# Expert 0's rows by one-hot products, earlier ranks, another order of the prologue

## The chip, the core and the metric

The kernel runs on one core of a Trainium2 chip. A core has engines that run their own instruction streams side by side: TensorE (PE, matrix products, with its weight loads shown apart as PEld), VectorE (DVE), ScalarE (ACT), GpSimd (POOL) and SyncE (SP), which here only issues transfers. Engines wait for each other on semaphores, and 16 DMA engines move data between main memory (HBM) and the core's SBUF. Matrix products accumulate in PSUM, which has eight banks. The metric is the time of one execution on the device, in microseconds (us); lower is better.

## What is computed

The reference is one step of a decoder layer on 512 prompt tokens and 8 sample tokens of 1024 numbers: three branches (convolution, stick-breaking attention, cross-attention to a memory), merged by gates, then a mixture of experts. The change touches the start (norm and first projections) and the experts:

```python
def rms_norm(x, g):
    xf = x.astype(jnp.float32)
    y = xf * lax.rsqrt(jnp.mean(xf * xf, axis=-1, keepdims=True) + EPS)
    return y.astype(x.dtype) * g
...
    e_logits = (hf @ w_router + b_router).astype(jnp.float32).reshape(T, N_GROUPS, EXPERTS_PER_GROUP)
    e_in = jnp.take_along_axis(e_logits, g_idx[:, None, None], axis=1)[:, 0]
    top_v, top_i = lax.top_k(e_in, TOP_K)
    gate = jax.nn.softmax(top_v, axis=-1) * jnp.take_along_axis(g_prob, g_idx[:, None], axis=1)
    expert = g_idx[:, None] * EXPERTS_PER_GROUP + top_i
...
        return (jax.nn.silu(xb @ w1[e]) * (xb @ w3[e])) @ w2[e]
```

Each token chooses one of 4 groups and in it 2 of 8 experts. There are 32 experts with w1 and w3 of 1024x512 and w2 of 512x1024, so 6 MB of float32 weights for each.

## The kernel before

Tokens are worked on in NT = 5 tiles: four of 128 prompt tokens (0 to 3) and one with the 8 sample tokens (4). D = 1024 is cut in KD = 8 slices k. Each engine has a program written out by hand, so the order of its instructions is that of the source; semaphores named in the source tie the engines together. Nothing is scheduled by a tool.

**Prologue.** SP loads the x tiles, then the first weight chunks and the small vectors; POOL makes the constants and loads page_i (the page table) over its own DMA queue, q0. For each tile in the order 4, 0, 1, 2, 3, ACT squares and sums a row (L1453) and takes the root (L1445, one tile behind the squares), DVE takes the reciprocal and scales the tile (L1807, L1808). PE turns the scaled tile by multiplying with ident (transposes, L754), ACT writes xn_hi (times norm1, rounded for the fast fp32r format) and DVE xn_lo, the rest. The projection is then a sum of three products, xn_hi by w_hi, xn_lo by w_hi and xn_hi by w_lo (three_products, L775); ACT and DVE split each weight chunk into w_hi (L1464) and w_lo (L1813). Chunks 0 and 1 are multiplied together, k by k; the transposes of slices 4 to 7 stand ahead of the products of slices 0 to 3.

**Router.** After the branches are merged and projected, the tiles go through the router in the order MERGE_TILES = 0, 1, 4, 2, 3. For each, PE turns x1 (turn_x) and multiplies by w_r (route_x, L1219), ACT writes the normed rows h_tok (scaled, L1701) and stores them to h_dram over its own queue (L1704), and DVE chooses the two experts (choose, L2205 to L2226), which ends in picked, a 0/1 row of 32 experts for each token. When the last tile is done, PE multiplies picked by triangles of ones (L1260, L1262), which gives every token's rank among those of its expert; DVE turns the ranks into positions (at_pos, one-hot over the CAP = 64 slots of an expert), and find (L1272) multiplies at_pos by pick_tok, the token numbers, so that each slot knows its token. DVE writes these as pair_row (L2266), and POOL gathers from h_dram the 128 rows of a pair of experts with an indirect DMA (gather, L702). keep_warm (L1226) are products whose result nobody reads. A second find with pick_of gives the gates of the slots; the over_ instructions on DVE and a third find (with over_pos) find tokens beyond 64 for an expert.

**Experts.** A pair's gathered rows xg are turned by PE in two halves through bank 4 (turn_rows), and DVE multiplies each half by norm2 into xg_t (rows_out, L2318). For each expert PE multiplies xg_t by w1 and w3 (up, L1304 and L1305), DVE copies that out (up_sb, L2352), PE turns it (turn_up), ACT applies the sigmoid (L1737) and DVE finishes the activation; PE multiplies by w2 (down, L1320 and L1321). ACT then scales the result by the gate: first few (L1743, for the sample tokens), then y_top (L1747); DVE makes y_rest (L2364). While the next expert runs, PE spreads the rows back to the tokens (give, L1330, by the one-hot spread that POOL writes, L711), and DVE adds them to x (L2369). The weights have three places, a, b and c, and expert n uses place n mod 3; SP issues w1 and w3 in halves of 1 MB and w2 with 2 MB as soon as the place is free (L533, L554, L558, L564). Expert 0's first loads are issued before the router ends.

## Time and profile before

| | us |
|---|---|
| runs (3) | 1096.79, 1097.74, 1098.09; median 1097.74 |
| profiled execution | 1102.6 |
| its span | 1100.8 |
| PE busy in the span | 1048.1 |

The profiled execution has a span (first to last instruction) of 1100.8 and its whole time is 1102.6. "PE busy" is the time with at least one product under way. The trace's times count from the start of the span. In the windows, PEclk is the clock that TensorE was granted, as a share of full speed (1.00 is 2.4 GHz, 0.50 is 1.2 GHz), and a DMA share of 1.00 means that all 16 DMA engines were busy. "Releaser" is what an instruction waited for last.

### The profile page before, as it was taken

What the parts mean: (1) busy time and instruction counts of PE and PEld (TensorE: products, weight loads), DVE (VectorE), ACT (ScalarE), POOL (GpSimd) and SP (SyncE); (2) the same over time, 40 slices, a digit from 0 to 9 for tenths busy, and PEclk for the clock granted to TensorE, in tenths of its full rate; (3) what the DMA queues carried; (4) which work ended last, traced back from release to release, by engine and by line L of the source; (5) the groups of instructions that cost most, each with busy time, mean ns of one, the idle gap of its engine ahead of it and who ended that gap; (6) DMA issues with size and microseconds to landing.
All of it is one profiled execution on the core that took longest, in us unless ns stands there. A gap on an engine that the chain in (4) does not pass through costs nothing.

```text
span 1100.8 us, 15991 instructions
## 1 busy us (share of the span) xinstructions
PE 1048.1 (95%) x6536; PEld 691.9 (63%) x6536; DVE 572.2 (52%) x913; ACT 307.7 (28%) x450; POOL 148.5 (13%) x179
## 2 busy tenths in 40 slices
PE   5999999999999999999998799999999999999995
PEld 4999987888867778899776344333444343433431
DVE  4312333677756855543545545556555655555555
ACT  5322211255436544322343011111111111111110
POOL 0000000001312565000000201111111011111110
PEclk9999999999999999999989799999999999999998
DMA  5622231544461243452415999999999999999962
GB/s 196 248 81 92 79 96 39 186 152 173 144 220 56 70 134 96 168 209 102 159 41 214 398 425 427 425 426 425 427 427 426 426 425 427 425 426 429 425 292 79
DMA packets 50213, 278.37 MB, mean 253 GB/s; under 512 B 7522, under 2 KB 7794, under 8 KB 29668
## 3 DMA queue, kind: packets, MB, share of 16 engines
q1 hardware_dynamic: 41332, 254.26, 57.3%
q0 software_dynamic: 6048, 16.86, 4.6%
q10 hardware_dynamic: 2768, 6.33, 1.6%
q8 instruction: 47, 0.77, 0.3%
q14 instruction: 18, 0.15, 0.0%
HBM read 274.04 MB, written 7.48 MB: 256 GB/s over the span
## 4 chain that ended last, share of the span: by engine, by line
PE 88%; DMA 4%; DVE 3%; issue 2%; POOL 1%; ACT 1%; SPq 0%; ACTq 0%; DVEq 0%; POOLq 0%
PE acc_all L775 25%; PE acc_all L1304 20%; PE acc_all L1320 10%; PE acc_all L1330 7%; PE acc_all L905 6%; PE acc_all L754 5%; PE acc_all L1153 4%; PE acc_all L836 2%; PE acc_all L955 1%; PE acc_all L1023 1%; DMA xg<-h_dram,pair_row 1%; DMA h_dram<-h_tok 1%; PE acc_all L1321 1%; DMA vals<-in_cache_mem_v 1%; DMA vals<-in_cache_v,page_row 1%
## 5 line engine op out<-in xcount | busy, mean ns | idle before, releaser
L775 PE MATMUL acc_all<-xn_hi,w_hi 128*128 128x260 f32 x832 | 173.9, 290 | 5.5 <-DVE gate_sb L1969 2.4
L775 PE MATMUL acc_all<-xn_hi,w_lo 128*128 128x260 f32 x832 | 168.6, 284 | 0.0
L775 PE MATMUL acc_all<-xn_lo,w_hi 128*128 128x260 f32 x832 | 168.1, 284 | 0.0
L2369 DVE TENSOR_TENSOR x<-x,acc_all 128x1024 f32<-128x1024 f32 x128 | 152.6, 1214 | 1.0 <-PE acc_all L1330 0.9
L775 PEld LDWEIGHTS acc_all<-xn_hi,w_hi 128*128 128x128 f32 x832 | 129.8, 190 | 14.9 <-issue 8.2
L775 PEld LDWEIGHTS acc_all<-xn_hi,w_lo 128*128 128x128 f32 x832 | 129.3, 190 | 0.0
L775 PEld LDWEIGHTS acc_all<-xn_lo,w_hi 128*128 128x128 f32 x832 | 129.3, 190 | 0.0
L711 POOL TENSOR_SCALAR spread<-tok_row,slots 128x512 fp32r<-128x512 f32 x32 | 50.1, 1566 | 380.7 <-PE acc_all L1330 380.7
L1813 DVE TENSOR_TENSOR w_lo<-w_raw,w_hi 128x1024 fp32r<-128x1024 f32 x52 | 63.4, 1221 | 67.6 <-ACT w_hi L1464 67.4
L1743 ACT ACTIVATE few<-acc_all,slots 8x512 f32<-8x512 f32 x64 | 43.4, 678 | 146.0 <-PE acc_all L1321 125.5
L1737 ACT ACTIVATE gate_h<-acc_all 128x256 f32<-128x256 f32 x32 | 12.3, 383 | 254.8 <-PE acc_all L754 254.8
L1304 PE MATMUL acc_all<-w_a,xg_t 128*64 128x512 f32 x176 | 80.4, 611 | 0.8 <-DVE xg_t L2318 0.8
L1305 PE MATMUL acc_all<-w_a,xg_t 128*64 128x512 f32 x176 | 80.4, 611 | 0.0
L2352 DVE COPY up_sb<-acc_all 128x512 f32<-128x512 f32 x32 | 22.1, 692 | 108.6 <-PE acc_all L1305 108.4
L1305 PE MATMUL acc_all<-w_b,xg_t 128*64 128x512 f32 x176 | 77.8, 595 | 0.0
L1304 PE MATMUL acc_all<-w_b,xg_t 128*64 128x512 f32 x176 | 77.8, 595 | 0.0
L2364 DVE SCALAR_TENSOR_TENSOR y_rest<-acc_all,slots,y_top 128x512 fp32r<-128x512 f32 x32 | 24.0, 751 | 93.0 <-ACT y_top L1747 93.0
L1305 PE MATMUL acc_all<-w_c,xg_t 128*64 128x512 f32 x160 | 70.8, 595 | 0.0
L1304 PE MATMUL acc_all<-w_c,xg_t 128*64 128x512 f32 x160 | 70.8, 595 | 0.0
L1330 PE MATMUL acc_all<-y_top,spread 64*128 64x512 f32 x256 | 60.9, 470 | 4.0 <-DVE x L2369 2.2
L1330 PEld LDWEIGHTS acc_all<-y_top,spread 64*128 64x128 f32 x256 | 24.0, 183 | 61.4 <-issue 28.5
L1472 ACT ACTIVATE proj<-acc_all 128x520 f32<-128x520 f32 (+1 forms) x28 | 16.9, 604 | 147.2 <-PE acc_all L775 141.1
(365 smaller groups left out, 1854.8 us busy)
## 6 DMA issues: line engine op xcount, KB each, us to landing
w_a<-in_w SPq DMA_DIRECT2D x44, 1024.0 KB, 16.4
w_b<-in_w SPq DMA_DIRECT2D x44, 1024.0 KB, 17.3
w_c<-in_w SPq DMA_DIRECT2D x40, 1024.0 KB, 17.8
w_raw<-in_w_in SPq DMA_DIRECT2D x52, 512.0 KB, 3.6
w_a<-in_w SPq DMA_DIRECT2D x11, 2048.0 KB, 17.4
w_b<-in_w SPq DMA_DIRECT2D x11, 2048.0 KB, 18.9
w_c<-in_w SPq DMA_DIRECT2D x10, 2048.0 KB, 20.4
w_br<-in_w_branch SPq DMA_DIRECT2D x24, 256.0 KB, 4.7
```

Of the source, the lines that this page charges most:

```text
L711: pool.tensor_scalar(spread[n % 2][:, :], tok_row[:, :], slot_tok[:, n:n + 1], None, ALU.is_equal).then_inc(spread_ok, 1)
L754: return pe.transpose(out, in_, ident[0:k, 0:k])
L775: mm = pe.matmul(out[:, a, :], w[:, slot, k, :], x[:, k, a * HALF_TOK:(a + 1) * HALF_TOK], start=first, stop=last)
L905: mm = pe.matmul(out[:, a, :], w, x[:, a * HALF_TOK:(a + 1) * HALF_TOK], start=begin, stop=end)
L1153: return pe.matmul(bank(MERGE_BANKS[i][half]), m[:, k, tok(tt)], w[:, k, half * 512:(half + 1) * 512], start=first, stop=last)
L1304: pe.matmul(bank(5)[0:CAP, :], lhs, w1_sb[w][:, k, :], start=(k == 0), stop=(k == KD - 1))
L1305: mm = pe.matmul(bank(5)[CAP:P, :], lhs, w3_sb[w][:, k, :], start=(k == 0), stop=(k == KD - 1))
L1320: pe.matmul(bank(7)[0:CAP, :], act_t[:, c, :], w2_sb[w][:, c, 0:DE], start=(c == 0), stop=(c == CW - 1))
L1330: mm = pe.matmul(bank(2 * pair + half), spread[hot][at, tok(t)], y[at, :], start=first, stop=not first)
L1743: act.activation(few[n // QUADS % 2][half][strip:strip + NB, :], bank(7)[at, :], ACT.Copy, scale=slot_gate[at, n:n + 1]).then_inc(few_in, 1)
L1813: dve.tensor_tensor(w_lo[:, slot, :, :], w_raw[:, slot, :, :], w_hi[:, slot, :, :].bitcast(F32), ALU.subtract).then_inc(split_lo, 1)
L2369: dve.tensor_tensor(x1[:, t, :], x1[:, t, :], bank(2 * pair, 2), ALU.add).then_inc(back_ok, 1)
```

## The change

What it does, engine by engine:

- **Rows of expert 0.** hot is a one-hot of slot against token for expert 0 alone. PE multiplies the rows h_tok, which lie in SBUF, by hot (hot_rows) and gets expert 0's rows already turned in banks 0 and 4; DVE multiplies by norm2 into xg_t. Expert 0 waits for row_sb and no more for the gather. Rows 0 to 63 of xg_t are filled this way; for expert 1 the pair's gathered rows are turned as before, but after expert 0's down products.
- **Ranks in two parts.** The ranks of the first four tiles (in ROUTE_TILES' order 4, 0, 1, 2) are multiplied before the last tile is chosen (rank_early), those of tile 3 after it (rank_late); slots, positions and find are cut in the same way.
- **Stores and gathers.** The last tile's row store goes from ACT's queue to SP's, ahead of w3[1]. The second half of w3 and w1 of place c waits for row_ps as well, since h_tok lies there. gather(1) waits until the second find (ids_ps 2), because at_pos now lies in its buffer.
- **Moves.** The second find stands behind expert 0's up products, the third behind its down products; the over_ instructions on DVE stand beside expert 0, and few_hot behind rows_out(0, 1). turn_rows(1, 1) and its rows_out stand at the end of expert 1 instead of in the middle of it. keep_warm is removed.
- **Prologue.** page_i is loaded after all x tiles are scaled. ACT's root follows each square at once, the last tile is scaled in two halves, chunk 1's split comes after slice 3, the products of chunk 0 for slices 0 to 3 come first, each followed by the transposes of slice k + 4, and then those of chunk 1. PE multiplies ident by itself (warm_up) 10 times at the start, 2 times behind each of the first three tiles and 5 times ahead of the first product.

The semaphores x1_ld and route_ld became one (late_ld); three new ones are h_ok (rows scaled), row_ps (late hot products) and row_sb. The diff, cut to its core, in the order SP, POOL, PE, ACT, DVE, with the common indentation taken off:

```diff
...
 sp.wait_ge(wo_ps, 2 * NT)
 load_up(0, 0, w1_sb, w1_d)
+sp.wait_ge(h_ok, NT)
+sp.dma_start(h_dram[tok(MERGE_TILES[NT - 1]), :], h_tok[:, MERGE_TILES[NT - 1], :]).then_inc(h_st, 16)
 load_up(1, 1, w3_sb, w3_d)
...
 sp.wait_ge(h_st, 16 * NT)
+sp.wait_ge(row_ps, 2)
 load_up(2, 2, w3_sb, w3_d)
...
-pool.dma_start(page_i[:, :], io["page_table"].rearrange("b j -> (b j)").partition_broadcast(P)).then_inc(page_ld, 16)
...
+pool.wait_ge(xn_ok, NT)
+pool.dma_start(page_i[:, :], io["page_table"].rearrange("b j -> (b j)").partition_broadcast(P)).then_inc(page_ld, 16)
 pool.wait_ge(rows_ok, 1)
...
 gather(0)
-gather(1)
 pool.wait_ge(ids_ok, 2)
 spread_block(0)
 spread_block(1)
...
-pool.wait_ge(dest_ok, 3)
+pool.wait_ge(ids_ps, 2)
+gather(1)
+pool.wait_ge(dest_ok, OVER_SET)
...
+def warm_up(times):
+    for _ in range(times):
+        pe.matmul(bank(0)[:, 0:P], ident[:, :], ident[:, :], start=True, stop=True)
+pe.wait_ge(consts, 1)
+warm_up(10)
...
 for tt in range(NT - 1):
     pe.wait_ge(xn_ok, tt + 2)
     for k in range(4):
-        mm = turn(bank(4 + k)[:, tok(tt)], x_in[:, tt, k * P:(k + 1) * P], P)
+        mm = turn_tile(tt, k)
         if tt == NT - 2:
             mm.then_inc(xt_ps, 1)
+    if tt < NT - 2:
+        warm_up(2)
...
+warm_up(5)
 pe.wait_ge(split_lo, 1)
-pe.wait_ge(xt_lo, 1)
-for k in range(KD):
+pe.wait_ge(xn_ok, NT + 1)
+for k in range(4):
     pe.wait_ge(xt_lo, k + 2)
-    if k + 4 < KD:
-        for tt in range(NT - 1):
-            mm = turn(bank(4 + k)[:, tok(tt)], x_in[:, tt, (k + 4) * P:(k + 5) * P], P)
-        mm.then_inc(xt_ps, 1)
     three_products(0, k, acc_pair(0))
-    pe.wait_ge(split_lo, 2)
+    for tt in range(NT - 1):
+        mm = turn_tile(tt, k + 4)
+    mm.then_inc(xt_ps, 1)
+pe.wait_ge(split_lo, 2)
+for k in range(4):
+    three_products(1, k, acc_pair(2))
+for k in range(4, KD):
+    pe.wait_ge(xt_lo, k + 2)
+    three_products(0, k, acc_pair(0))
     mm = three_products(1, k, acc_pair(2))
 mm.then_inc(w_used, 2)
...
-keep_warm(3)
...
-o = bank(1)[:, 0:(NT + 1) * NE]
-pe.matmul(o, tri_bf[:, :], picked[:, :, :], start=True, stop=False, skip_group_check=True)
-for back in range(1, NT + 1):
-    mm = pe.matmul(o[:, back * NE:], ones_bf[:, :], picked[:, 0:NT + 1 - back, :], start=False, stop=(back == NT),
-                   skip_group_check=True)
-mm.then_inc(rank_ps, 1)
...
-keep_warm(1)
-pe.wait_ge(dest_ok, 1)
-find(at_pos, lambda n, r, c: pick_tok[0:n, r, c, :], NE, bank(3))
-keep_warm(2)
-pe.wait_ge(dest_ok, 2)
-find(at_pos, lambda n, r, c: pick_of[0:n, r, c, :], NE, bank(2))
-keep_warm(2)
...
+def rank_early():
+    o = bank(1)
+    pe.matmul(o[:, 0:LAST * NE], tri_bf[:, :], picked[:, 0:LAST, :], start=True, stop=False, skip_group_check=True)
+    for back in range(1, NT + 1):
+        n = min(LAST, NT + 1 - back)
+        mm = pe.matmul(o[:, back * NE:(back + n) * NE], ones_bf[:, :], picked[:, 0:n, :], start=False, stop=False,
+                       skip_group_check=True)
+    mm.then_inc(rank_ps, 1)
...
+def rank_late():
+    o = bank(1)
+    pe.matmul(o[:, LAST * NE:NT * NE], tri_bf[:, :], picked[:, LAST, :], start=False, stop=False,
+              skip_group_check=True)
+    pe.matmul(o[:, NT * NE:(NT + 1) * NE], ones_bf[:, :], picked[:, LAST, :], start=False, stop=True,
+              skip_group_check=True).then_inc(rank_ps, 1)
...
+def hot_rows(half, tiles):
+    for kk in range(KD // 2):
+        k = KD // 2 * half + kk
+        for r in tiles:
+            tt = ROUTE_TILES[r]
+            n = rows(tt)
+            mm = pe.matmul(bank(4 * half)[:, kk * CAP:(kk + 1) * CAP], h_tok[0:n, tt, k:D:KD], hot[0:n, r, :],
+                           start=(kk == 0 and r == 0), stop=(r == LAST), skip_group_check=True)
+    return mm
...
+early, late = range(LAST), range(LAST, NT)
+merge_out(4, 1, range(KD // 2, KD))
+route_x(4, 0)
+pe.wait_ge(pick_ok, LAST)
+rank_early()
+turn_x(4, 1)
+route_x(4, 1)
+pe.wait_ge(dest_ok, HOT_EARLY)
+pe.wait_ge(h_ok, LAST)
+hot_rows(0, early)
+hot_rows(1, early)
+pe.wait_ge(dest_ok, POS_EARLY)
+pe.wait_ge(pick_ok, NT)
+rank_late()
+pe.wait_ge(pick_ok, NT + 1)
+find_ids(early)
+pe.wait_ge(dest_ok, HOT_LATE)
+pe.wait_ge(h_ok, NT)
+for half in range(2):
+    hot_rows(half, late).then_inc(row_ps, 1)
+pe.wait_ge(dest_ok, POS_LATE)
+find_ids(late).then_inc(ids_ps, 1)
...
-turn_rows(0, 0)
-turn_rows(0, 1)
 for n in range(NE):
...
-    if j == 0:
+    if n >= 1:
         pe.wait_ge(xgt_sb, 2 * p + 2)
-    if n >= 1:
         pe.wait_ge(up_ok, n)
-    up_and_gate(n % WS, p % 2, j, n // WS + 1)
+    up_and_gate(n % WS, p % 2, j, n // WS + 1, first=(n == 0))
     if n >= 1:
         give(n - 1, (0, 1))
     else:
-        pe.wait_ge(dest_ok, 3)
-        find(over_pos, lambda m, r, c: over_in[0:m, r, c, :, :].rearrange("p a b -> p (a b)"), 2 * EXTRA, bank(0))
+        pe.wait_ge(dest_ok, GATED)
+        find(at_pos, lambda m, r, c: pick_of[0:m, r, c, :], NE, bank(2)).then_inc(ids_ps, 1)
...
-    if n + 2 < NE:
+    if n == 1:
+        turn_rows(1, 0)
+    elif 2 <= n < NE - 2:
...
     down(n % WS, n // WS + 1, n)
+    if n == 0:
+        pe.wait_ge(dest_ok, OVER_SET)
+        find(over_pos, lambda m, r, c: over_in[0:m, r, c, :, :].rearrange("p a b -> p (a b)"), 2 * EXTRA,
+             bank(0)).then_inc(ids_ps, 1)
+        turn_rows(0, 0)
+        turn_rows(0, 1)
     if 1 <= n < NE - 1:
         give(n - 1, (3,))
+    if n == 1:
+        turn_rows(1, 1)
...
     act.activation(junk[0:n, :], x_in[0:n, t, :], ACT.Square, accum_out=ss[0:n, t:t + 1]).then_inc(sumsq_ok, 1)
-    if i >= 1:
-        root(i - 1)
-root(NT - 1)
+    if i == NT - 1:
+        act.wait_ge(xst_f, 1)
+        act.activation(xn_hi[:, :, SEQ:TOK], xst_tmp[:, :, :], ACT.Copy).then_inc(xt_hi, 1)
+    root(i)
...
 split_chunk(0)
-act.wait_ge(xst_f, 1)
-act.activation(xn_hi[:, :, SEQ:TOK], xst_tmp[:, :, :], ACT.Copy).then_inc(xt_hi, 1)
-split_chunk(1)
 act.wait_ge(norm_ld, 16)
 for k in range(KD):
+    if k == 4:
+        split_chunk(1)
     act.wait_ge(xt_ps, k + 1)
...
-    act.dma_start(h_dram[tok(tt), :], h_tok[0:n, tt, :]).then_inc(h_st, 16)
+    act.activation(h_tok[0:n, tt, :], x1[0:n, tt, :], ACT.Copy, scale=rs2[0:n, i:i + 1]).then_inc(h_ok, 1)
+    if i < NT - 1:
+        act.wait_ge(h_ok, i + 1)
+        act.dma_start(h_dram[tok(tt), :], h_tok[0:n, tt, :]).then_inc(h_st, 16)
...
-mean_square(0)
 for i, t in enumerate(START_TILES):
     n = rows(t)
-    if i + 1 < NT:
-        mean_square(i + 1)
+    mean_square(i)
...
-    dve.tensor_scalar(x_in[0:n, t, :], x_in[0:n, t, :], rs[0:n, t:t + 1], None, ALU.mult).then_inc(xn_ok, 1)
+    if i < NT - 1:
+        dve.tensor_scalar(x_in[0:n, t, :], x_in[0:n, t, :], rs[0:n, t:t + 1], None, ALU.mult).then_inc(xn_ok, 1)
+    else:
+        for half in range(2):
+            at = slice(half * D // 2, (half + 1) * D // 2)
+            dve.tensor_scalar(x_in[0:n, t, at], x_in[0:n, t, at], rs[0:n, t:t + 1], None, ALU.mult).then_inc(xn_ok, 1)
+    if i == NT - 2:
...
+def hot_slots(r0, r1, part):
+    dve.wait_ge(rank_ps, part + 1)
+    at, n = slice(r0, r1), r1 - r0
+    link(dve.scalar_tensor_tensor(out=hot_rank[:, at], in0=picked[:, at, 0], scalar=-float(NO_TOKEN),
+                                  in1=rank[:, at, 0], op0=ALU.mult, op1=ALU.add))
+    dve.tensor_tensor(hot[:, at, :], bc(hot_rank[:, at].unsqueeze(2), [P, n, CAP]),
+                      bc(pos_low[:, :].unsqueeze(1), [P, n, CAP]), ALU.is_equal).then_inc(dest_ok, 1)
...
+def rank_picked(r0, r1):
+    at, n = slice(r0, r1), r1 - r0
+    link(dve.tensor_tensor(pick_of[:, at, :, :], bc(rank[:, at, :].unsqueeze(2), [P, n, 2, NE]), pick[:, at, :, :],
+                           ALU.mult))
...
+hot_slots(0, LAST, 0)
+rank_picked(0, LAST)
 dve.wait_ge(sumsq_ok, NT + 2 + 6)
 dve.scalar_tensor_tensor(out=rs2[:, 4:5], in0=ss2[:, 4:5], scalar=EPS * D, in1=ss2_b[:, 0:1], op0=ALU.add,
                          op1=ALU.add).then_inc(ms_ok, 1)
+rank_sum(0, LAST)
 scale2(2, slice(4, 5))
+position(0, LAST)
 choose(4)
...
-dve.tensor_tensor(pick_tok[:, :, :, :], pick[:, :, :, :], bc(tok_f[:, :].unsqueeze(2).unsqueeze(3), choice), ALU.mult)
+dve.tensor_tensor(pick_tok[:, :, :, :], pick[:, :, :, :], bc(tok_f[:, :].unsqueeze(2).unsqueeze(3), choice),
+                  ALU.mult).then_inc(pick_ok, 1)
+hot_slots(LAST, NT, 1)
+rank_picked(LAST, NT)
+rank_sum(LAST, NT)
+position(LAST, NT)
...
+for half in range(2):
+    ks = slice(KD // 2 * half, KD // 2 * (half + 1))
+    dve.wait_ge(row_ps, half + 1)
+    if half == 0:
+        dve.wait_ge(lg_ps, NT)
+        dve.wait_ge(lg_max, 1)
+    dve.tensor_tensor(xg_t[:, 0, ks, 0:CAP], bank(4 * half)[:, 0:KD // 2 * CAP].rearrange("p (k t) -> p k t", k=KD // 2),
+                      bc(norm2_pk[:, ks].unsqueeze(2), [P, KD // 2, CAP]), ALU.mult).then_inc(row_sb, 1)
...
     else:
+        over_first()
+    dve.wait_ge(sig_ok, n + 1)
+    if n >= 1:
+        dve.wait_ge(y2_ps, n)
+    act_out(2 * n)
+    if n == 0:
+        dve.wait_ge(ids_ps, 2)
+        dve.tensor_copy(slot_gate[:, 0:NE], bank(2)[:, 0:NE]).then_inc(ids_ok, 1)
+        over_rest()
+        rows_out(0, 0)
+        rows_out(0, 1)
         dve.wait_ge(ids_ps, 3)
         link(rows_found(PAIRS, EXTRA // 2, bank(0)))
...
-    if n + 2 < NE:
...
+    elif n == 1:
+        rows_out(1, 0)
+    elif n + 2 < NE:
         rows_out(n // 2 + 1, n % 2)
...
     y_rest_out(slot_gate[:, n:n + 1])
     if 1 <= n < NE - 1:
         added(n - 1, (3,))
+    if n == 1:
+        rows_out(1, 1)
...
```

On PE, from the end of the router to expert 0, these stood in a row before (xg_168 is a gathered pair; w13_ld0a the first halves of w1 and w3 in place a):

```order
L1219 MATMUL acc_all<-w_r,x_t_163 128x36 [waits ht_sb]
L1226 MATMUL acc_all<-x_105,ident 128x512 x3
L1260 MATMUL acc_all<-picked,tri_bf 128x192 [waits pick_ok]
L1262 MATMUL acc_all<-picked,ones_bf 128x160
L1272 MATMUL acc_all<-pick_tok,at_pos 64x32 [waits dest_ok]
L1272 MATMUL acc_all<-pick_of,at_pos 64x32 [waits dest_ok]
L754 MATMUL acc_all<-ident,xg_168 128x128 [waits xg_ld0]
L754 MATMUL acc_all<-ident,xg_168 128x128 [waits xgt_sb]
L1304 MATMUL acc_all<-w_a,xg_t 64x512 [waits w13_ld0a,xgt_sb]
```

On PE at the same place, these stand there now (L1316 are the hot products):

```order
L1294 MATMUL acc_all<-picked,tri_bf 128x128 [waits pick_ok]
L1249 MATMUL acc_all<-w_r,x_t_163 128x36 [waits ht_sb]
L1316 MATMUL acc_all<-hot,h_tok 128x64 [waits h_ok,dest_ok]
L1316 MATMUL acc_all<-hot,h_tok 128x64 x31
L1304 MATMUL acc_all<-picked,tri_bf 128x32 [waits pick_ok,dest_ok]
L1283 MATMUL acc_all<-pick_tok,at_pos 64x32 [waits pick_ok]
L1316 MATMUL acc_all<-hot,h_tok 128x64 x7
L1283 MATMUL acc_all<-pick_tok,at_pos 64x32 [waits dest_ok]
L1365 MATMUL acc_all<-w_a,xg_t 64x512 [waits w13_ld0a,row_sb]
L1283 MATMUL acc_all<-pick_of,at_pos 64x32 [waits dest_ok]
```

The transposes of the gathered rows are gone from the place ahead of expert 0's first up product, the hot products stand there instead, and the gates' find has moved behind the up products.

On DVE, in expert 1, these stood in a row before (xg_t is the half of the next pair's rows, x_105 is x1, y_rest that of expert 1):

```order
L2318 TENSOR_TENSOR xg_t<-acc_all,norm_pk 128x512 [waits xgt_ps]
L2369 TENSOR_TENSOR x_105<-x_105,acc_all 128x1024 [waits back_ps] x2
L2364 SCALAR_TENSOR_TENSOR y_rest<-acc_all,slots,y_top 128x512 [waits top_ok]
L2369 TENSOR_TENSOR x_105<-x_105,acc_all 128x1024 [waits back_ps]
L2352 COPY up_sb<-acc_all 128x512 [waits upt_ps,up_ps]
```

On DVE at the same place, these stand there now:

```order
L2448 TENSOR_TENSOR xg_t<-acc_all,norm_pk 128x512 [waits xgt_ps]
L2476 TENSOR_TENSOR x_105<-x_105,acc_all 128x1024 [waits back_ps] x2
L2471 SCALAR_TENSOR_TENSOR y_rest<-acc_all,slots,y_top 128x512 [waits top_ok]
L2476 TENSOR_TENSOR x_105<-x_105,acc_all 128x1024 [waits back_ps]
L2448 TENSOR_TENSOR xg_t<-acc_all,norm_pk 128x512 [waits xgt_ps]
L2459 COPY up_sb<-acc_all 128x512 [waits upt_ps,up_ps]
```

A second xg_t, the other half of expert 2's and 3's rows, now stands behind y_rest of expert 1 and one more addition.

On SP, at the router's end, these transfers now stand in a row; the store to h_dram is the new one, and the last row has row_ps as a second wait:

```order
L539 DMA w_a<-in_w 128x2048 [waits wo_ps]
L560 DMA h_dram<-h_tok 128x1024 [waits h_ok]
L539 DMA w_b<-in_w 128x2048 x2
L562 DMA w_b<-in_w 128x4096
L539 DMA w_c<-in_w 128x2048 x2
L539 DMA w_c<-in_w 128x2048 [waits row_ps,h_st]
```

The store stands between expert 0's w1 and expert 1's w3, so everything from w3[1] on is issued behind it.

## Rows read from the trace of the kernel before

**Rows 1.** The page, part 1: busy us (share of the span) xinstructions of each engine.

```profile
PE 1048.1 (95%) x6536; PEld 691.9 (63%) x6536; DVE 572.2 (52%) x913; ACT 307.7 (28%) x450; POOL 148.5 (13%) x179
```

**Rows 2.** Chain of waits, 590 to 630: start us, us, what.

```profile
595.37 9.12 DMA h_dram<-h_tok
...
605.35 9.20 DMA xg<-h_dram,pair_row
...
617.73 0.70 DVE xg_t L2318
...
619.60 0.85 PE acc_all L1304
...
624.20 0.43 PE acc_all L1304
```

**Rows 3.** Windows, 614 to 616: PE, PEld, DVE, ACT, POOL busy (x), PEclk, DMA share, GB/s.

```profile
614.00:616.00 2.00, 1.12 (x4) 0.71 (x4) 0.17 (x1) 0.00 (x0) 0.00 (x0) 0.50 0.98 404
```

**Rows 4.** Tiles w_b, w_c: duration ns min/median/max, first and last start us, forms.

```profile
L1304 PE MATMUL acc_all<-w_b,xg_t x176: 592/592/643, 634.8 to 1074.8; 128*64 128x512 f32 x176
...
L1304 PE MATMUL acc_all<-w_c,xg_t x160: 592/592/643, 649.1 to 1046.1; 128*64 128x512 f32 x160
```

**Rows 5.** DMA issues, 1010 to 1027: xcount, KB each, median us from issue to landing.

```profile
w_a<-in_w SPq DMA_DIRECT2D x1, 2048.0 KB, 28.9
```

**Rows 6.** Timeline, 1000 to 1070: start us, us, engine, line, operation [idle before <-releaser].

```profile
1024.72 0.33 SPq L564 DMA_DIRECT2D w_a<-in_w  x1
...
1064.09 0.61 PE L1320 MATMUL acc_all<-w_a,act_t 128*64 128x512 f32 x1 [0.31 <-DVE act_t L2361]
```

**Rows 7.** Timeline, prologue (0 to 36), ACT, DVE and PE.

```profile
10.05 1.06 ACT L1453 ACTIVATE junk<-x_in 128x1024 f32<-128x1024 f32 x1 [2.47 <-DMA x_in<-in_x_prompt]
...
15.91 1.23 DVE L1813 TENSOR_TENSOR w_lo<-w_raw,w_hi 128x1024 fp32r<-128x1024 f32 x1
...
18.68 0.78 PE L775 MATMUL acc_all<-xn_hi,w_hi 128*128 128x260 f32 x2
...
19.26 0.64 PE L775 MATMUL acc_all<-xn_lo,w_hi 128*128 128x260 f32 x2
...
23.00 0.40 PE L775 MATMUL acc_all<-xn_hi,w_lo 128*128 128x260 f32 x2
```

**Rows 8.** Windows, 7.0 to 7.5, columns as in rows 3.

```profile
7.00:7.50 0.50, 0.08 (x1) 0.11 (x2) 0.27 (x1) 0.50 (x3) 0.00 (x0) 1.00 2.21 141
```

**Rows 9.** DMA queues, 6 to 8: packets, MB, share of 16 engines.

```profile
q0 software_dynamic: 20, 0.01, 51.6%
```

**Rows 10.** Timeline, router's end (590 to 626).

```profile
593.92 1.08 PE L1219 MATMUL acc_all<-w_r,x_t 128*128 128x36 f32 x8 [0.69 <-ACT x_t L1686]
...
598.77 0.18 DVE L2226 TENSOR_TENSOR picked<-pick 128x32 bf16<-128x32 bf16 x1
...
601.48 1.47 PE L1272 MATMUL acc_all<-pick_tok,at_pos 8*64 8x32 f32 x40 [1.05 <-DVE at_pos L2260]
```

**Rows 11.** DMA issues, 560 to 600, columns as in rows 5.

```profile
w_a<-in_w SPq DMA_DIRECT2D x2, 1024.0 KB, 5.9
```

**Rows 12.** Windows, DVE's work between pair_row and over_pos, columns as in rows 3.

```profile
603.00:612.50 9.50, 6.83 (x48) 2.92 (x48) 8.58 (x30) 0.00 (x0) 5.15 (x4) 0.82 1.01 425
618.30:623.30 5.00, 4.83 (x12) 1.48 (x14) 4.62 (x14) 0.00 (x0) 0.00 (x0) 0.50 1.03 437
```

**Rows 13.** Timeline, POOL and DVE at 607 to 611.

```profile
607.71 3.13 POOL L711 TENSOR_SCALAR spread<-tok_row,slots 128x512 fp32r<-128x512 f32 x2
607.80 2.21 DVE L2300 TENSOR_TENSOR scan<-scan 128x32 f32<-128x32 f32 x4
```

**Rows 14.** Timeline, behind expert 1's last down product (648 to 652).

```profile
648.58 1.38 ACT L1743 ACTIVATE few<-acc_all,slots 8x512 f32<-8x512 f32 x2 [4.48 <-PE acc_all L1321]
...
650.71 0.75 DVE L2364 SCALAR_TENSOR_TENSOR y_rest<-acc_all,slots,y_top 128x512 fp32r<-128x512 f32 x1 [2.59 <-ACT y_top L1747]
...
651.38 1.21 DVE L2369 TENSOR_TENSOR x<-x,acc_all 128x1024 f32<-128x1024 f32 x1
```

175 lines of the change are left out of this document (89 added, 86 removed).

## The prediction

> **What bounds the kernel now.** I read the page first: TensorE (PE) is busy for 1048.1 of 1100.8 us [rows 1], so time can only come out of the few places where PE stands or runs at its lower clock. The chain of waits names the largest. The last row store is issued at 595.37 and needs 9.12 us, because it queues behind weights; the gather that reads it back needs another 9.20; then come transposes and two multiplications by the norm weights, the second 0.70 [rows 2]. While PE waited it idled, and the windows show what followed: a granted clock of 0.50, the lower of its two levels (1.2 of 2.4 GHz) [rows 3]. At that level a pair of expert products takes 0.85 us, later 0.42 to 0.43 [rows 2]. The first six pairs of expert 0 run so, which costs 6 x 0.43 = 2.5 us. Experts 1 and 2 begin at 634.8 and 649.1 [rows 4], so an undisturbed expert takes 14.3.
>
> Second, the weights: could they refuse an earlier expert stage? Expert 30's w2 is issued at 1024.72 [rows 6] and takes 28.9 [rows 5], so it is there at 1053.6; its first use is at 1064.09 [rows 6]. That slack of 10.5 us is the most that the expert stage can be moved ahead. Third, the prologue: the first product begins at 18.68, and products run at the lower level until about 22.8 (0.64 us for two that overlap, later 0.40) [rows 7].
>
> **Prologue.** The square of x tile 2 waited 2.47 us for its DMA and began at 10.05 [rows 7], while ACT had been ready at 7.58. In that stretch transfers fell to 141 GB/s [rows 8], and q0, which holds only the page table's load then, took 51.6% of the 16 engines with 20 packets [rows 9]. The change issues that load after the last x tile is scaled; its first reader, a gather of key pages, comes late in the attention, so the delay is hidden. The Trainium skill speaks against a gain here: "DMA: Bandwidth & Descriptors", section "SWDGE vs HWDGE vs iDMA", says that each DMA engine goes round-robin between the queues of either kind, so 20 small packets should hardly delay x. By that rule the 1.75 us below would drop out and the whole sum would be 8.0 instead of 9.7; the rows of this place show the opposite.
>
> With ACT's root now placed right after each square, I put tile 2's square at 8.3, 1.75 sooner. Chunk 1's split no longer stands before the first xn_lo (1.23 [rows 7]), and the transposes of k = 4 no longer stand before the first product (0.7, the gap from the last xn_lo to 18.68). Some 0.2 more comes from scaling the last tile in halves. So the first product starts at 18.68 - 1.75 - 1.23 - 0.7 - 0.2 = 14.8. Not all is kept: the 0.46 us of those transposes return behind the first product, and pacing by xn_lo (ACT 0.69, DVE 0.75 for each k) I estimate at 0.3. The clock decides the rest. Before, 4.1 us of products passed before the rise, costing 2.0. The warm-ups put some 1.35 us of work straight ahead of the first product, so I let the rise come after 2.75 us of products, which cost 1.35. Gain: 3.9 - 0.46 - 0.3 + 0.65 = **3.8**. If products run at the full level at once it is 5.1. The trace has no warm-ups; 3 us of transposes before 18.68 did not raise the clock, so the other end is that the lower level lasts through the four interleaved k (2.45 us each, against 1.2): 1.3 slower. Everything up to the router is paced by PE, so this carries on.
>
> **Router to expert 0** (times of the trace of before). The early ranks are six small bf16 products, about 0.5, at 592. On DVE the early slots (two instructions, estimated 0.7) and rank_picked (estimated 0.42, four of the five tiles) come ahead of the reciprocal and push the last choose, which ended at 598.95 [rows 10], by 0.2 to 0.4. The early hot products are 32 of 128x64: from eight router products of 36 columns in 1.08 [rows 10] I take 0.135 each, 4.3 us, with 3.4 as the other end. They run from 595.0 to 599.3, beside choose, which hides them. Then follow pick_tok 0.49, slots of the last tile 0.4, eight late hot products 1.0, and two halves of the norm multiplication at 0.42 (of which PE waits for the first only): expert 0 starts at **601.75** instead of 618.48. Its w1 halves land 5.9 us after 590.94 [rows 11], so at 596.9, which is no limit. Store and gather leave the path: the store now stands ahead of w3[1] on SP and waits for h_ok at 595.9; behind it are queued w3[1], w2[1] and w1[2], a gap of at most 0.5 us in a stream that still holds w1[0]; the gather lands at about 612.4. The gather of experts 2 and 3 waits for a product after expert 0's up and lands at 620, used at 629.
>
> **Expert 0 to 1.** What was 16.7 sooner is not kept. The up products take 16 x 0.43 = 6.9, to 608.65, but DVE's routing work now stands beside expert 0 instead of before it, and expert 1 needs xg_t, which comes behind it. In the trace this work is the 9.5 and 5.0 us of two windows [rows 12]; less few_hot (1.1, moved behind), plus up_out 0.69 and act_out 1.13, it takes 15.2 from 602.3, so over_pos ends at 617.5 (616.65 if the scan steps beside POOL's spread run at their usual pace). Then find 1.47 [rows 10], and two times transposes 0.6 and multiplication 0.70 through one bank, with gaps: expert 1 starts at **621.8** instead of 634.8, 13.0 sooner. A rule of the skill bears on the same row: beside two POOL spreads (3.13) four scan steps took 2.21 on DVE [rows 13], some 1.3 more than such a step costs elsewhere. "SBUF — State Buffer", section "Who interferes with whom", says that a DVE instruction with two SBUF inputs and a GpSimd one that reads SBUF exclude each other wholly; by that, up to 3.13 instead would be lost, expert 1 would start at 623.0, and the sum would be 1.2 smaller. The row shows less.
>
> **Expert 1 to 2: a new wait.** Expert 2 needs the second half of its pair's rows, whose transposes now stand at the end of expert 1, and on DVE their multiplication stands behind y_rest of expert 1 and a 1.21 us addition [rows 14]. y_rest needs ACT's two "few" (1.38) and y_top, all after the last down product. In the trace of before, those steps lie beside expert 2: 648.58 to 651.38 + 1.21 = 652.6 [rows 14]; with 0.70 for the multiplication and gaps, expert 2's first product comes 4.95 us after the end of down(1), where it was 0.65. So 4.3 of the 13.0 are given back: expert 2 starts at 640.4, **8.7** sooner. During the stall PE idles for about 4 us, as it did ahead of expert 0 in before, where the lower level followed. I take one such fall at its measured price of 2.5, and 0.3 for the spread of the terms: **5.9** of 8.7. With no fall 8.5 to 9; with two (one more behind expert 0) 3.4. All is under the 10.5 that the weights allow. From expert 2 on nothing differs.
>
> **Sum.** 3.8 + 5.9 = 9.7. The profiled execution took 1102.6, so it would be 1092.9; the median of the runs is 1097.74, which gives **1088.0**.
>
> **Rivals.** (1) *The clock holds*: prologue 5.1, experts 8.5, together 13.6, 1084.1. For it: expert 0 now follows the router's products almost without a gap; against it: the stall before expert 2. (2) *The clock falls twice, or rises late in the prologue*: 3.4 from the experts and between -1.3 and 1 from the prologue, 2.1 to 4.4 in all: 1093.3 to 1095.6. For it: the transposes that raised nothing. (3) *Slower*: the lower level holds from the hot products on. They would take 32 x 0.28 = 9.0 instead of 4.3 (4.7 later), and the up products of expert 0 13.8 instead of 6.9, to 620.3; with both finds (1.5 each), turning and activating (1.5), down (3.4) and the two bank turns (2.9), expert 1 starts at 631.1; its up products take another 6.9 more and the stall 4.3: expert 2 at 631.1 + 14.3 + 6.9 + 4.3 = 656.6, 7.5 later than before. With the late prologue (1.3) that is 1106.5. It decides once more than 12.5 us (8.7 + 3.8) are lost; against it, PE is busy nearly throughout from 594 to 608. (4) *The change does not do what it says*: expert 0 still waits for weights; then only the prologue is left, 1094; the 5.9 us to landing [rows 11] speak against it. (5) *The page table's load did not hold x up*: x comes no sooner, the 1.75 drops out, 9.7 - 1.75 = 7.95 is left: 1089.8, inside the forecast's spread.
>
> **How the numbers follow.** Forecast, with (5) in it, 0.56; (1) 0.17; (2) 0.19; (3) 0.04; (4) 0.04. The range leaves out the slow case, half of (2)'s upper side and what lies below (1): 1083 to 1094.5. A measurement of this kernel tells 0.2% (2.2 us) from no change. Faster than that holds the forecast, (1), (4) and most of (2): 0.92; within it, the top of (2): 0.04; slower, (3): 0.04.
>
> **What would show it.** Right: tile 2's square near 8.3 and the first product near 14.8; two 128x260 products falling from 0.64 to 0.40 by 17.5; expert 0 starting 16.7 + 3.8 sooner, expert 1 16.8, expert 2 some 10 to 12.5; ahead of expert 2 PE idle for about 4 us with DVE's xg_t as its releaser. Wrong: a granted clock of 0.50 under the hot products, PE waiting for a weight DMA in expert 0 or the last experts, or an x tile as late as before.

## The result: 0.8% slower, where 0.9% faster was forecast

The changed kernel took 1105.34 us (median of 4 runs, 1104.60 to 1106.99); the kernel before took 1097.91. The ratio is 1.0079, with an interval of 1.0061 to 1.0097. The profiled execution took 1105.24 with a span of 1103.4, so this time it stands at the median; the profiled execution of before stood 4.9 above its own.

TensorE is busier than in [rows 1], in part 1 of the page of the changed kernel (busy us, share, instructions):

```profile
PE 1065.0 (97%) x6644; PEld 715.9 (65%) x6644; DVE 573.7 (52%) x923; ACT 307.7 (28%) x450; POOL 149.0 (14%) x180
```

17 us more for 108 more instructions: what was added is dear, and it isn't waiting. The up products of the three weight places show from where on the time is lost (w_a holds expert 0, w_b expert 1, w_c expert 2; ns min/median/max, first and last start; compare [rows 4]):

```profile
L1365 PE MATMUL acc_all<-w_a,xg_t x176: 592/592/1094, 612.7 to 1062.8; 128*64 128x512 f32 x176
L1365 PE MATMUL acc_all<-w_b,xg_t x176: 592/592/643, 633.1 to 1077.1; 128*64 128x512 f32 x176
L1365 PE MATMUL acc_all<-w_c,xg_t x160: 592/592/643, 651.6 to 1048.4; 128*64 128x512 f32 x160
```

Place a in the kernel before:

```profile
L1304 PE MATMUL acc_all<-w_a,xg_t x176: 592/592/1115, 618.5 to 1060.5; 128*64 128x512 f32 x176
```

Expert 0 begins 5.8 sooner than in the profile of before (612.7 against 618.48), expert 1 only 1.7 sooner, expert 2 begins 2.5 later. Forecast were 20.5, 16.8 and 12.5 sooner (the prologue's 3.8 included). From expert 2 on nothing differs, as the prediction said.

The prologue is not at fault. The square of x tile 2, the first two products and the copy of the first chunk, from the timeline:

```profile
7.75 1.04 ACT L1521 ACTIVATE junk<-x_in 128x1024 f32<-128x1024 f32 x1
...
14.04 0.48 PE L800 MATMUL acc_all<-xn_hi,w_hi 128*128 128x260 f32 x2 [0.27 <-DVE xn_lo L1905]
14.36 0.40 PE L800 MATMUL acc_all<-xn_lo,w_hi 128*128 128x260 f32 x2
...
27.55 0.60 ACT L1541 ACTIVATE proj<-acc_all 128x520 f32<-128x520 f32 x1 [6.03 <-PE acc_all L800]
```

Against [rows 7], the square starts 2.3 sooner, the first product 4.6 sooner, and two products take 0.40 from the second on where they took 0.64: the clock is up at once. The first chunk is copied out at 27.55, in before at 33.62:

```profile
33.62 0.60 ACT L1472 ACTIVATE proj<-acc_all 128x520 f32<-128x520 f32 x1 [4.58 <-PE acc_all L775]
```

The loss stands in the chain of waits behind the router (start us, us, what):

```profile
588.01 18.26 PE acc_all L1316 x64
606.32 1.99 PE acc_all L1283 x32
608.32 4.00 PE acc_all L1316 x16
...
613.79 0.85 PE acc_all L1365
...
617.34 0.43 PE acc_all L1365
...
627.87 0.83 DVE over_pos L2443
...
651.60 0.64 PE acc_all L1365
```

L1316 are the hot products. The early ones hold PE for 18.26 us, where 4.3 were forecast; the late ones take 4.00, where 1.0 was forecast. The store and the gather [rows 2] are gone from the chain, as intended, but they took 18.3 of it, and the products that replace them take 22.3. The windows give the clock there (columns as in [rows 3]):

```profile
588.00:590.00 2.00, 2.00 (x9) 1.88 (x8) 1.67 (x9) 1.70 (x2) 0.00 (x0) 0.58 1.00 422
...
600.00:604.00 4.00, 4.00 (x16) 3.63 (x15) 0.00 (x0) 0.00 (x0) 0.00 (x0) 0.50 1.00 424
608.00:610.00 2.00, 2.00 (x14) 1.94 (x12) 0.00 (x0) 1.29 (x2) 0.00 (x0) 0.50 0.01 4
648.00:651.00 3.00, 0.20 (x2) 0.01 (x1) 1.94 (x3) 1.00 (x2) 1.23 (x1) 1.00 1.05 445
```

PE counts as busy without a gap and yet runs at the lower level, from 588.3 to 615.6. In the stall ahead of expert 2 (the last row) it is the reverse: PE stands and the clock holds. At 608 to 610 the transfers have stopped too, since w3[2] now waits for the hot products; in 600 to 612 their share is 0.57, in before 1.01. No product later waited for a weight.

### The profile page after: what moved, and what is told of

It reads as the page before. It is cut to its first block, busy times and chain, and to the rows that moved or that the text cites. A ratio compares the mean times of both kernels' runs of the same rounds, so it can differ in the third digit from the quotient of the medians.

```text
span 1103.4 us, 16224 instructions
## 1 busy us (share of the span) xinstructions
PE 1065.0 (97%) x6644; PEld 715.9 (65%) x6644; DVE 573.7 (52%) x923; ACT 307.7 (28%) x450; POOL 149.0 (14%) x180
## 4 chain that ended last, share of the span: by engine, by line
PE 89%; DVE 4%; DMA 2%; ACT 2%; issue 2%; POOL 1%; ACTq 0%; SPq 0%; DVEq 0%; POOLq 0%
PE acc_all L800 25%; PE acc_all L1365 20%; PE acc_all L1381 10%; PE acc_all L1391 7%; PE acc_all L935 5%; PE acc_all L767 5%; PE acc_all L1183 4%; PE acc_all L866 2%; PE acc_all L1316 2%; PE acc_all L985 1%; DMA vals<-in_cache_mem_v 1%; PE acc_all L1053 1%; PE acc_all L1382 1%; PE acc_all L1249 1%; DMA vals<-in_cache_v,page_row 1%
## 5 line engine op out<-in xcount | busy, mean ns | idle before, releaser
L1805 ACT ACTIVATE gate_h<-acc_all 128x256 f32<-128x256 f32 x32 | 12.3, 383 | 246.5 <-PE acc_all L767 246.5
## 6 DMA issues: line engine op xcount, KB each, us to landing
w_a<-in_w SPq DMA_DIRECT2D x44, 1024.0 KB, 14.9
w_c<-in_w SPq DMA_DIRECT2D x10, 2048.0 KB, 16.6
```

## Experiments

**The reference point.** The kernel before, unchanged, was run once more, since its profiled execution was 4.9 above its median and the prediction's sum was made against that execution.

> The kernel before, unchanged, for a second profile. The profiled execution that the prediction read took 1102.6 us, 4.7 us above the median of the runs (1097.9). Theory 1: that execution was an unlucky one, in which TensorE's granted clock lay at its lower level through the first part of expert 0; most executions have it at the full level there, so a second profile shows a span near 1096 with expert 0 at 0.43 us per pair from its first pair on. Theory 2: the lower level at expert 0 belongs to every execution and the profile itself costs the 4.7 us: span near 1100.8 again, first pairs of expert 0 at 0.85 us.

Measured: 1097.69, ratio 0.9994 (0.9977 to 1.0011), span 1095.6. The square of x tile 2 in its timeline, and the up products of w_b:

```profile
8.78 1.06 ACT L1453 ACTIVATE junk<-x_in 128x1024 f32<-128x1024 f32 x1 [1.30 <-DMA x_in<-in_x_prompt]
```

```profile
L1304 PE MATMUL acc_all<-w_b,xg_t x176: 592/592/643, 632.6 to 1072.5; 128*64 128x512 f32 x176
```

The lower clock under expert 0 is there again (610.8 to 621.0), so both expectations fell: neither a missing fall nor a fixed span explains the 4.9. The same program differs by execution in two places. Tile 2's wait was 1.30 this time, 2.47 before, and the first chunk came 1.6 sooner. From the last instruction on DVE to the end of the span it took 1.9, before 4.8. All further comparisons of times inside the span use this profile where it says so.

**The prologue alone.** Before, with the new prologue and nothing else of the change.

```diff
+pe.wait_ge(consts, 1)
+warm_up(10)
...
+pool.wait_ge(xn_ok, NT)
+pool.dma_start(page_i[:, :], ...)
...
-            root(i - 1)
+        root(i)
```

> The kernel before with the new prologue alone (page table's load after the x tiles, root right after each square, warm-ups, products of chunk 0 first); routing and experts as before. In the changed kernel the two chunks ended at 27.5 us instead of 33.6. Theory 1: everything from there to the router is paced by TensorE, so the 6.1 us carry to the end: 1091.8 us. Theory 2: a later stage is paced by transfers (key pages, values, or the experts' weights) and gives the gain back: 1096 to 1098 us.

Measured: 1091.58, ratio 0.9935 (0.991 to 0.996). The first products run at the full level (14.87 0.40, below). The first chunk is out at 28.07, against 32.03 in the second profile of before, and expert 0 starts at 611.1 against 616.5; here are the up products of place a, first with the new prologue, then in that profile:

```profile
L1322 PE MATMUL acc_all<-w_a,xg_t x176: 592/592/1116, 611.1 to 1053.5; 128*64 128x512 f32 x176
```

```profile
L1304 PE MATMUL acc_all<-w_a,xg_t x176: 592/592/1115, 616.5 to 1058.2; 128*64 128x512 f32 x176
```

The time is the first theory's 1091.8. By the medians the prologue brings some 6.5 us (by the interval 4.4 to 9.9), more than the 3.8 of the forecast; by these two traces it brings 4.0 at the first chunk and 4.7 at the last instruction on DVE. The rest of the change costs 13.8.

**Where the prologue's gain is from.** First its warm-ups left out, then the page table's load put back to its old place, each in the kernel with the prologue alone.

```diff
-pe.wait_ge(consts, 1)
-warm_up(10)
...
-        if tt < NT - 2:
-            warm_up(2)
...
-    warm_up(5)
```

> pro_only without the warm-up products. Theory 1: the warm-ups are what raises the granted clock ahead of the first product (in the changed kernel every product runs at the full level); without them the first products run at 0.64 us a pair again for some 3 to 4 us and the transposes ahead of them at the lower level too, and the end comes 1.5 to 2.5 us later: 1093 to 1094 us. Theory 2: the earlier x tiles and the closer order raise it as soon: 1091.6 us.

Measured: 1094.8, ratio 0.9979 (0.995 to 1.0008). The second pair of products, without warm-ups and with them (one line of each timeline):

```profile
14.70 0.64 PE L779 MATMUL acc_all<-xn_lo,w_hi 128*128 128x260 f32 x2
```

```profile
14.87 0.40 PE L788 MATMUL acc_all<-xn_lo,w_hi 128*128 128x260 f32 x2
```

Without them the products start 0.4 sooner (14.12), at the lower level, and the first chunk comes out at 29.68 instead of 28.07. By the medians the warm-ups are worth 3.2 of the 6.5 us, a little more than the first theory expected. But the two intervals overlap, and the traces don't show it at the end. The 1.6 us are down to 0.2 at 129 us: PE falls to the lower level at about 120 us in both, for 6.8 us with the warm-ups and 3.4 without. Expert 0 then starts 1.0 sooner without them (with them at 611.1, above):

```profile
L1312 PE MATMUL acc_all<-w_a,xg_t x176: 592/592/1115, 610.1 to 1052.4; 128*64 128x512 f32 x176
```

Its span is longer (1092.7 against 1090.9) only by what follows the last instruction on DVE, 2.9 us more. So the warm-ups raise the clock at the first products; what of it reaches the end is not shown.

```diff
+pool.dma_start(page_i[:, :], ...).then_inc(page_ld, 16)
 pool.iota(row_f[:, :], ...)
...
-pool.wait_ge(xn_ok, NT)
-pool.dma_start(page_i[:, :], ...).then_inc(page_ld, 16)
```

> pro_only with the page table's load back at its old place, ahead of the x tiles' arrival. Theory 1: this load held up x tiles 2 and 3 (in the kernel before the square of tile 2 waited 2.47 us for its transfer); tile 2 comes at 10 again instead of 7.75 and all of the prologue is about 2 us later: 1093.5 us. Theory 2: the x tiles were late for another reason, and the load costs nothing here: 1091.6 us.

Measured: 1091.23, ratio 0.994 (0.9922 to 0.9958), the same as without this edit. The squares of x tiles 2 and 3 in its timeline:

```profile
8.05 1.06 ACT L1470 ACTIVATE junk<-x_in 128x1024 f32<-128x1024 f32 x1
...
10.38 1.06 ACT L1470 ACTIVATE junk<-x_in 128x1024 f32<-128x1024 f32 x1 [0.76 <-DMA x_in<-in_x_prompt]
```

With the page table's load at its old place tile 2 needed no wait, and tile 3 one of 0.76. In the time of the whole kernel the load's place makes no difference that can be measured, as the second theory said. But that theory's reason does not hold: the transfers show that the load does hold x up. Their rate in 40 equal slices of 2 to 9 us, first with the load at its old place, then with it moved:

```profile
GB/s 0 117 23 23 164 211 94 187 515 351 398 398 421 398 421 421 515 398 398 375 257 398 492 421 445 424 401 351 331 228 108 53 47 47 47 94 47 25 140 259
```

```profile
GB/s 0 70 47 0 47 234 164 281 351 445 492 398 375 398 398 375 445 445 468 445 351 398 421 374 468 445 445 445 375 398 421 374 445 445 408 314 425 468 445 374
```

Between 7 and 9 us the mean is 98 to 159 GB/s in all three profiles with the load at its old place (both of before and this one), and 395 to 418 in all eleven with it moved. Which x tile is caught differs: tile 2 waited 2.47 and 1.30 in the two profiles of before, tile 3 0.76 here, where the first product came 0.46 later than with the load moved (15.01 against 14.55).

**The last row store alone.** The prologue, and the last store issued from SP ahead of w3[1].

```diff
+    sp.wait_ge(h_ok, 1)
+    sp.dma_start(h_dram[tok(MERGE_TILES[NT - 1]), :], h_tok[:, MERGE_TILES[NT - 1], :]).then_inc(h_st, 16)
     load_up(1, 1, w3_sb, w3_d)
```

> pro_only with one part of the routing change: the last tile's row store is issued by SP ahead of expert 1's w3 and not from ACT's queue; gather, ranks and experts as before. In pro_only the store took 8.65 us and was there at 597.4; the gather was issued at 598.28, while the row numbers that it needs were ready at 596.7. Theory 1: the store was only some 0.7 us later than those numbers, so its own 9 us were mostly hidden beside choosing and ranking, and the gather's 8.9 us stay: at most 1 to 1.5 us, 1090 to 1091.6 us. Theory 2: the store's 9 us and, by less queueing, part of the gather's stood on the path: 4 us or more, 1087.5 us or less.

Measured: 1088.16, ratio 0.9908 (0.9889 to 0.9928); the interval overlaps that of the prologue alone. The chain of waits of the prologue alone, then that with the store moved:

```profile
588.75 8.65 DMA h_dram<-h_tok
...
598.28 8.92 DMA xg<-h_dram,pair_row
```

```profile
595.88 0.17 DVE pair_row L2295
...
597.08 8.99 DMA xg<-h_dram,pair_row
```

The store has left the chain, and the router's own work has taken its place, so the gather is issued only 1.2 sooner; expert 0 begins at 610.0 instead of 611.1. The medians say 3.4, the starts of expert 0 say 1.1: how much the store's place is worth stays open between these, as the time lies between the two expectations.

**The early hot products left out.** The changed kernel without them, so that expert 0's rows of tiles 0, 1, 2 and 4 are missing.

```diff
...
-    hot_rows(0, early)
-    hot_rows(1, early)
```

> The changed kernel without the 32 early hot products (tiles 4, 0, 1 and 2 are left out of expert 0's rows; all else runs). In the changed kernel they fill TensorE from 588.0 to 606.3. Theory 1: they are the cost that the prediction put at 4.3 us; without them the last choose (picked at 591.7) sets the pace and expert 0 starts at 597 to 600 instead of 612.7: 1105.3 - 13 to -16 = 1089 to 1092 us. Theory 2: what is late is the lower clock that sets in at 588 whatever runs there, and the chain behind it; then at most half of that comes, 1097 to 1101 us.

Measured: 1090.46, ratio 0.9918 (0.9881 to 0.9954): 14.9 us off the changed kernel, and expert 0 starts at 598.2 instead of 612.7. That is the time expected, and it settles where the time went:

```profile
L1363 PE MATMUL acc_all<-w_a,xg_t x176: 592/592/1094, 598.2 to 1052.8; 128*64 128x512 f32 x176
L1363 PE MATMUL acc_all<-w_c,xg_t x160: 592/592/1061, 639.6 to 1038.4; 128*64 128x512 f32 x160
```

It also shows how little the rest of the routing change is worth: the prologue alone took 1091.58. Against that kernel expert 0 starts 12.9 sooner here, but expert 1 follows 21.3 later (there 16.6) and expert 2 another 20.1 (there 14.3), so that expert 2 starts only 2.4 sooner (639.6 against 642.0). The run doesn't yet say why 32 products take 18 us.

**Is it the clock?** Three products of 128 x 512 straight ahead of the hot products, to raise it.

```diff
     pe.wait_ge(h_ok, LAST)
+    for _ in range(3):
+        pe.matmul(bank(5), ident[:, :], x1[:, 0, 0:512], start=True, stop=True)
     hot_rows(0, early)
```

> The changed kernel with three of the old keep-warm products (128x512, whose result nobody reads; 2.8 us at the full level) put straight ahead of the early hot products. In the changed kernel the granted clock falls at 588.1, when these begin, and stays at 0.50 until 615.4. Theory 1: the hot products themselves hold the lower level, so it sets in a few us later and lasts as before: 1104 to 1107 us. Theory 2: the gaps between 584.7 and 587.9 made it fall, and with the gaps filled it stays at the full level: 32 products in 9 us instead of 18.3, and the late ones, finds and first up products faster too: 1105.3 + 2.8 - 9.2 - 4.8 = 1094 us.

Measured: 1109.86, ratio 1.0108 (1.0085 to 1.0131), some 3 us above what the first theory expected; its kind was right. Its line of early hot products in the timeline, and windows of L1316 alone (us, PE busy (x), PEld busy (x), PEclk, DMA share, GB/s):

```profile
587.74 18.06 PE L1316 MATMUL acc_all<-hot,h_tok 8*128 8x64 f32 x64
```

```profile
588.00:592.00 4.00, 4.00 (x16) 3.80 (x16) 1.00 1.01 426
594.00:598.00 4.00, 4.00 (x15) 3.53 (x15) 0.50 0.98 412
```

The clock was raised and held until 593.4. A window counts every instruction that reaches into it: 16 in four microseconds at the full level, 15 at the lower. So the clock doesn't price these instructions. Nor do they keep it up: with PE busy throughout, it fell in the midst of them and stayed low until 617.3. In this run's profile the lower level also set in behind the stall ahead of expert 2, for some 6 us, which the profile of the changed kernel was spared; whether the 3 us above the expectation are these is not shown.

**Is it the number of instructions?** The rows and the one-hot blocks were given the type fp32r, so that low bits of the rows are lost.

```diff
-        h_tok = place("h_tok", "ys", 0, [NT, D])
+        h_tok = place("h_tok", "ys", 0, [NT, D], F32R)
...
-        hot = place("hot", "ys", 20480, [NT, CAP])
+        hot = place("hot", "ys", 20480, [NT, CAP], F32R)
...
```

> The changed kernel with h_tok and hot written in the rounded fp32r format, in which a product is one instruction and not two (the rows of all experts lose their low bits by that). In the changed kernel each instruction of the hot products takes 0.285 us at the lower level, and there are 64 for the 32 early products. Theory 1: the count of instructions is the cost: 32 in 9.1 us, the late ones in 2 instead of 4: 1105.3 - 9.2 - 2 = 1094 us, less if the clock rises sooner. Theory 2: what costs is loading each 128x128 block once, whatever the format: the time of an instruction doubles, 1104 to 1106 us.

Measured: 1093.55, ratio 0.9952 (0.9928 to 0.9977), as expected if instructions are the price. Early and late hot products:

```profile
587.11 9.83 PE L1316 MATMUL acc_all<-hot,h_tok 8*128 8x64 f32 x32
...
598.95 2.12 PE L1316 MATMUL acc_all<-hot,h_tok 128*128 128x64 f32 x8
```

The same 32 and 8 products are now 32 and 8 instructions instead of 64 and 16, and take half as long. A plain fp32 product is two instructions here.

**Is it the loaded block's step?** A hot product loads 128 columns h_tok[:, k:D:KD], every eighth value. Here it loads neighbouring ones, so that expert 0's columns are permuted; the three products of 512 columns stay.

```diff
...
-                        mm = pe.matmul(bank(4 * half)[:, kk * CAP:(kk + 1) * CAP], h_tok[0:n, tt, k:D:KD], hot[0:n, r, :],
+                        mm = pe.matmul(bank(4 * half)[:, kk * CAP:(kk + 1) * CAP], h_tok[0:n, tt, k * P:(k + 1) * P], hot[0:n, r, :],
...
```

> hot_warm with one change: the block of h_tok that is loaded for a hot product is 128 neighbouring numbers of a row and not every eighth (so expert 0's rows come out with their columns permuted). In hot_warm the 64 instructions came every 0.28 us on average and every 0.24 at the closest, at the full clock level as at the lower one, and each load took 0.334 us; the router's products, whose blocks lie together, came every 0.12 us at the full level. Theory 1: the step of 32 bytes between the loaded numbers sets the pace; without it the early products take 8 to 11 us instead of 18.1 and expert 0 starts 7 to 11 us sooner: 1109.9 - 7 to -11 = 1099 to 1103 us. Theory 2: the step does not matter, the products are paced by something else: 17 us or more again, 1108 us or more.

Measured: 1102.82, ratio 1.0067 (1.0043 to 1.0092), within the first theory's range. Two of that theory's steps fell short all the same: the early products took 13.1 us where 8 to 11 were expected, and expert 0 starts 4.5 sooner than with the step, not 7 to 11. The rest of the gain lies behind it: expert 2 starts 5.8 sooner, and the stretch at the lower level that follows is shorter. Its weight loads, then those of the changed kernel and those of the router in the kernel before (ns min/median/max), each from its trace:

```profile
L1316 PEld LDWEIGHTS acc_all<-hot,h_tok x80: 181/288/337, 588.5 to 606.8; 128*128 128x128 f32 x64, 8*128 8x128 f32 x16
```

```profile
L1316 PEld LDWEIGHTS acc_all<-hot,h_tok x80: 307/334/337, 587.9 to 611.8; 128*128 128x128 f32 x64, 8*128 8x128 f32 x16
```

```profile
L1219 PEld LDWEIGHTS acc_all<-w_r,x_t x80: 88/192/338, 568.4 to 594.7; 128*128 128x128 f32 x64, 128*8 128x8 f32 x16
```

And windows of L1316 with neighbouring columns, at either level of the clock:

```profile
589.00:593.00 4.00, 4.00 (x30) 3.60 (x30) 1.00 1.03 417
594.00:598.00 4.00, 4.00 (x17) 3.53 (x17) 0.50 1.04 438
```

At the full level 30 instructions stand where 16 stood with the step; at the lower level the two are near each other, 17 and 15. So the step takes away what the full clock would give, and either of them alone, step or lower level, makes an instruction dear. The early hot products went from 18.06 to 13.11 us because the clock held for their first 4.7 us; then it fell here too (593.1).

**The wait ahead of expert 2.** The changed kernel, with the second half of the next pair's rows turned before the last quarter of down(1) and multiplied earlier on DVE.

```diff
-    down(n % WS, n // WS + 1, n)
+    down(n % WS, n // WS + 1, n, between=(lambda: turn_rows(1, 1)) if n == 1 else None)
...
-    if n == 1:
-        turn_rows(1, 1)
...
+    if n == 1:
+        added(0, (1,))
+        rows_out(1, 1)
+        added(0, (2,))
```

> The changed kernel with one thing undone in another form: the second half's transposes for experts 2 and 3 stand ahead of the last quarter of expert 1's down products, and their multiplication on DVE between the two additions of expert 0's rows, so expert 2 no longer waits for y_rest of expert 1. Theory 1: the 3.4 us of waiting and the rest of the 18.5 us between the first products of experts 1 and 2 go down to 14.3 to 15: 1105.3 - 4 = 1101.3 us. Theory 2: expert 2 is then late for another reason, w3 of place c, whose load waits for the last hot products: still 17 us or more between them, 1104 us or more.

Measured: 1102.0, ratio 1.0037 (1.0019 to 1.0055). Expert 2's up products:

```profile
L1365 PE MATMUL acc_all<-w_c,xg_t x160: 592/592/643, 647.8 to 1044.8; 128*64 128x512 f32 x160
```

Expert 1 starts at 632.6, so expert 2 follows 15.2 later, in the changed kernel 18.5, and the time is that expected. The stall of 3.3 us is avoidable, and 3.3 by the medians is what it cost.

**A better form.** The operands change places: the one-hot block (now 64 slots of expert 0 and 64 of expert 1) is loaded, and the rows stream 512 wide. Four early tiles and two halves are 8 products instead of 32, there is no step in the loaded block, and both experts' rows come from SBUF, so the first gather goes. The result is copied to xg_0, turned and multiplied as gathered rows are. DVE's count of full experts stands ahead of it, and the turns ahead of expert 2 as in the run before.

```diff
-                for kk in range(KD // 2):
-                    ...
-                        mm = pe.matmul(bank(4 * half)[:, kk * CAP:(kk + 1) * CAP], h_tok[0:n, tt, k:D:KD], hot[0:n, r, :],
+                for r in tiles:
+                    ...
+                    mm = pe.matmul(bank(4 * half), hot[0:n, r, :, :].rearrange("p a b -> p (a b)"),
+                                   h_tok[0:n, tt, half * 512:(half + 1) * 512],
...
-            gather(0)
...
+            dve.wait_ge(row_ps, 1)
+            dve.tensor_copy(xg[0][:, 0:512], bank(0)).then_inc(row_sb, 1)
```

> Another form of the same idea on the new prologue: hot has the 128 slots of experts 0 and 1 and is the operand that is loaded, the rows h_tok are the one that streams, 512 numbers wide, two products for each tile; the result is the gathered form of the pair, copied out by DVE and ACT, turned and multiplied by norm2 like any pair; the gather of that pair is left out, and the transposes for experts 2 and 3 stand as in rows_mid. Theory 1: ten products of 0.94 us (as the keep-warm products of that form took at the full level), eight of them beside the last choose; expert 0 starts at 600 to 602 instead of 612.7, expert 1 17 us later, expert 2 14.5 after that: 651.6 - 632.5 = 19 sooner than in the changed kernel, 1086 to 1087 us. Theory 2: the weights' transfers or a fallen clock take half of that back: 1091 us or more.

Measured: 1082.21, ratio 0.9853 (0.983 to 0.9875), some 4 us better than expected. Its products in the timeline, and their loads:

```profile
584.88 6.97 PE L1313 MATMUL acc_all<-h_tok,hot 8*128 8x512 f32 x8
...
591.83 5.61 PE L1313 MATMUL acc_all<-h_tok,hot 8*128 8x512 f32 x12
```

```profile
L1313 PEld LDWEIGHTS acc_all<-h_tok,hot x20: 181/190/337, 584.9 to 596.4; 128*128 128x128 f32 x16, 8*128 8x128 f32 x4
```

Twenty instructions in 12.6 us move the rows of two experts, where eighty in 22.3 moved those of one. The wide ones lift the clock themselves: 8 in 6.97 at the lower level, then 12 in 5.61 at the full one. Experts 0, 1 and 2 start at 600.1, 615.9 and 631.0, expert 2 15.9 sooner than in the second profile of before. Against the prologue alone that is 11.0 at expert 2 and 9.4 by the medians. What each of the parts brings (the exchanged operands, both experts' rows, the gather left out, the order on DVE, the turns ahead of expert 2) was not measured apart.

One addition: two short products that nobody reads, of 128 and 320 columns, ahead of the early ranks and behind the last tile's turns, to keep the clock up.

```diff
     route_x(4, 0)
+    pe.matmul(bank(5)[:, 0:128], ident[:, :], x1[:, 0, 0:128], start=True, stop=True)
...
     turn_x(4, 1)
+    pe.matmul(bank(0)[:, 0:320], ident[:, :], x1[:, 0, 0:320], start=True, stop=True)
```

> pair_rows with two short products that nobody reads, of 128 and 320 columns, in the two gaps of TensorE ahead of the early ranks and behind the last tile's transposes (0.27 and 0.69 us in pair_rows). In pair_rows the granted clock lies at 0.50 from 584.2 to 591.0, under the first of the wide hot products. Theory 1: the gaps made it fall; filled, the level holds and 6.8 us of products take 3.4 less: 1079 us. Theory 2: the fall comes from what ran before these gaps, and nothing is gained: 1082 to 1083 us.

Measured: 1080.74, ratio 0.9864 (0.9841 to 0.9887). In the profiled execution the clock held:

```profile
583.47 3.89 PE L1313 MATMUL acc_all<-h_tok,hot 8*128 8x512 f32 x8
```

That is 3.1 us less for the same eight instructions. The intervals of the two ratios overlap, so whether the addition helps in the median stays open (expert 2 starts 2.9 sooner in its trace). Both beat the kernel before by 1.4 to 1.5%, and the changed one by over 2%.

## Why the prediction was wrong

**The step that failed** is the price of the early hot products: "from eight router products of 36 columns in 1.08 [rows 10] I take 0.135 each, 4.3 us". Two things were wrong in it.
- The x8 of that row counts instructions, and they are four products: half of the eight k of one tile. The eight early hot products of a tile are sixteen instructions, the 32 are 64 (the run in fp32r). By the same row the sum would have been 64 x 0.135 = 8.6. "FP8 and Floating Point Precision" of the Trainium skill, section "TensorE Precision Notes", says that a true fp32 product takes four passes through the array; the trace shows the cost as twice the instructions.
- The router's row stands for loads of neighbouring columns at the full level. The hot products load every eighth value, 32 bytes apart, and ran at the lower level; either is enough. Their load takes 0.334 (median) instead of 0.192, and one instruction 18.1 / 64 = 0.283 instead of 0.135. "Advanced Engine Details and Errata" of the Trainium skill, section "SBUF Cachelines", says that accesses which each touch another 16-byte line are penalised; the run with neighbouring columns agrees at the full level, 30 instructions against 16 in 4 us, and hardly shows such a penalty at the lower one (17 against 15).

Together 64 x 0.283 = 18.1 instead of 32 x 0.135 = 4.3. The cover failed with it: choose, beside which they were to run, wrote its last bits at 591.71, and they ended at 606.3 (timeline of the changed kernel):

```profile
591.71 0.17 DVE L2299 TENSOR_TENSOR picked<-pick 128x32 bf16<-128x32 bf16 x1
```

With the actual prologue (6.1 sooner than in the profile of before) the forecast end was 593.2, so 13.1 were lost there; the late ones add 3.0. Expert 0 is late by 17.0 (forecast 595.7 with that prologue, measured 612.7), and the last 0.9 lies mostly in the find between them: 32 instructions in 1.99 at the lower level, where 40 took 1.47 [rows 10].

The cover was not the whole of it. With the early hot products left out, the routing change brings 1.1 us by the medians, within the noise, where 5.9 were forecast. The late hot products and the finds, dearer than forecast, stand there too, the first five pairs of expert 0 run at the lower level, and so do 3.4 us behind the stall.

**Rival (3) named the consequence, at 0.04.** It put the lower level from the hot products on and priced them at 0.28 each. The level did set in there, which was also the prediction's own sign of being wrong. But the level was not the price: these instructions cost as much at the full level (the run with three wide products ahead). The argument against it, "PE is busy nearly throughout", was the wrong reading: busy time is no sign of a high clock. Nor do the hot products bring the first fall by themselves, as the windows of the run without the early ones and of the kernel before show (columns as in [rows 3]):

```profile
586.00:600.00 14.00, 9.75 (x71) 8.06 (x72) 7.63 (x36) 3.88 (x5) 0.35 (x1) 0.50 1.03 430
```

```profile
586.00:600.00 14.00, 11.11 (x66) 8.06 (x63) 8.56 (x39) 4.79 (x10) 0.65 (x2) 1.00 0.65 244
```

In before the wide keep_warm products stood in this stretch. The change removed them, and the prediction put that at nothing; no run put them back alone. The rival's further terms did not come: the level rose at 615.6, after three pairs of wide products at 0.85.

**Prologue: right in direction, by the medians too small.** 3.8 forecast, 6.5 measured, above the 5.1 of rival (1), though the traces show only 4.0 to 4.7. The clock term was too small: the full level held from the first products on, where a rise after 2.75 us was assumed. How much of that reaches the end is not shown (the run without warm-ups). The 1.75 for the page table's load had the cause right and the size wrong: the load does hold x up, against rival (5), but with the rest of the new prologue its place moved the first product by 0.46 and the median not measurably. In the old prologue it was not moved alone. The rule from "DMA: Bandwidth & Descriptors" of the Trainium skill, section "SWDGE vs HWDGE vs iDMA", that each DMA engine goes round-robin between the queues, does not foretell what was measured: with the load at its old place q0 took 51.6% of the engines' time with 20 packets [rows 9], and all transfers together fell from some 400 GB/s to 159 or less. Two sums of the prediction do not come out of their own figures. "1.3 slower" should be some 0.1 faster: four k at 1.25 more cost 5.0, which is 3.0 more than the 2.0 before, against 3.14 gained. And 3.13 instead of 1.3 lost beside POOL's spreads makes 1.8, not 1.2. Neither enters the sum of the forecast.

**Expert 0 to 1: right.** 20.05 later forecast, 20.4 measured. **Expert 1 to 2: right.** 18.6 forecast, 18.5 measured, with the releaser that was named (waits of the changed kernel, 583 to 655: total us, times, longest):

```profile
PE acc_all L1365 <- DVE xg_t L2448: 4.2, 2, 3.4
...
PE acc_all L1283 <- DVE over_pos L2443: 0.5, 1, 0.5
```

over_pos kept PE waiting for 0.5. **The clock fall of 2.5 behind that stall did not come** in the changed kernel's profile. It came in the four other kernels that keep that stall: about 3.4 us at the lower level where the early hot products were left out, in the fp32r run and in that with neighbouring columns, and some 6 us in that with three wide products. So the term isn't wrong in kind, and that one profile was spared it is no sign against it; what decides it was not shown.

**Weights: right.** The new wait on row_ps did cost transfers, the share of 0.01 at 608 to 610, and no product waited for a weight, within the slack that the prediction named.

**From the execution to the median.** Against the span the forecast missed by 12.3 (1091.1, from 1100.8 less 9.7, against 1103.4), against the median by 17.3. The other 5 is the 4.9 that was taken off because the profiled execution of before stood that much above its median. One part of that is the end of the span: from DVE's last addition to the end 4.8 there, 5.1 in the changed kernel, 1.9 in the second profile of before. It was 1.9 to 2.5 in eight of the fourteen profiles and 4.6 to 5.1 in six, with before in both groups, so it isn't put down to an edit. What decides it stays open; so some 3 us of the 7.4 are not explained by the change. 4.7 are: expert 2 starts at 651.6 against 646.9.

## What to carry to other kernels

Before pricing a product by a row, see whether the row counts products or instructions, and whether the loaded operand has the same type and step. When rows are picked by a one-hot product, load the one-hot block and stream the data wide: here that is a quarter of the instructions, no step in the load, and twice the rows. A PE that is busy throughout with narrow products may still be at its lower clock, and a few unread wide products ahead of the real ones can raise it for them (3.1 us at the wide hot products in one profile); whether that reaches the end has to be measured.

## What the runs showed of the chip

- A plain fp32 product was two instructions, one in fp32r: 64 in 18.1 us, then 32 in 9.83.
- A load of 128 x 128 fp32 with a 32-byte step took 0.307 to 0.338 us, whatever the level of the clock; with neighbouring columns 0.181 to 0.337, the low end at the full level.
- With PE busy without a gap in 64-column products behind 128-column loads, the granted clock fell from 1.00 to 0.50 and stayed there (hot products behind three wide ones: from 593.4 to 617.3). It rose again under the 512-column up products behind them (changed kernel: at 615.6).
- With a small load over q0 (20 packets) ahead of the x tiles' arrival, all transfers together fell to 98 to 159 GB/s for 2 us, in three profiles of three; without it they stayed at 395 to 418, in eleven of eleven.
- Between two executions of the kernel before, the arrival of x tile 2 differed by 1.3 us, and the time from the last instruction on DVE to the end of the span by 2.9 us.
